# A hybrid decoder layer on one core: seven tiles of x turned in 32-wide blocks on VectorE instead of transposed on TensorE

## What is computed

```python
def in_proj(x, ln_g, w_in):
    u = rmsnorm(x, ln_g) @ w_in                      # 1024 -> 512 + 128 + 128 + 512 + 512
    q, k, v, xl, yg = jnp.split(u, SPLITS, axis=-1)
    ...

q, k, v, xl, yg = in_proj(hp, ln1_g[l], w_in[l])
attn, kw, vw = swa_prompt(rotary(q, pos), rotary(k, pos), v, attn_sinks[l])   # window 128, 8 heads, 2 kv heads
lru_h, cbuf, hT = rglru(xl, conv0, h0, *lru_w)
hp = merge_and_ffn(hp, attn, lru_h, yg, *tail_w)     # output projection, router, 32 experts, top 2
```

## Time and profile before

| | us |
|---|---|
| median of 3 runs | 866.26 |
| the runs | 863.41, 866.26, 869.72 |
| profiled execution, its time | 867.14 |
| profiled execution, its span | 865.4 |
| mean granted clock of TensorE | 0.929 |

### The profile page before, as it was taken

One profiled execution on the slowest core, in us unless ns is written; L12 is line 12 of the kernel. 1 busy time (PEld: TensorE's weight loads), 2 busy tenths in 40 slices (PEclk: granted clock), 3 DMA queues, 4 the chain that ended last, 5 costly groups with the idle time before them and its releaser, 6 DMA issues.

```text
span 865.4 us, 11816 instructions
## 1 busy us (share of the span) xinstructions
PE 752.7 (87%) x4461; PEld 375.7 (43%) x4461; DVE 364.8 (42%) x1023; ACT 239.6 (28%) x556; POOL 140.9 (16%) x193
## 2 busy tenths in 40 slices
PE   6999999599999989899999259999999999999400
PEld 3666665256666645455555223333333333333100
DVE  0556665554458454565565711111111111111087
ACT  2766665400531534111111101111111111111022
POOL 1011001000121121021121221221122211221132
PEclk9999999698999989999999669999999999999855
DMA  9201200210110012611214648999999999992193
GB/s 335 103 25 49 105 7 1 101 53 0 55 37 19 1 48 92 279 73 51 95 50 172 266 115 294 416 395 420 409 404 417 405 420 406 399 376 96 65 388 142
DMA packets 28055, 164.10 MB, mean 190 GB/s; under 512 B 7017, under 2 KB 8193, under 8 KB 17738
## 3 DMA queue, kind: packets, MB, share of 16 engines
q1 hardware_dynamic: 19778, 145.34, 42.4%
q0 software_dynamic: 8080, 17.51, 5.5%
q10 hardware_dynamic: 144, 0.52, 0.2%
HBM read 151.14 MB, written 23.12 MB: 201 GB/s over the span
## 4 chain that ended last, share of the span: by engine, by line
PE 76%; DVE 10%; issue 5%; DMA 4%; ACT 4%; ACTq 0%; POOL 0%; DVEq 0%; SPq 0%; POOLq 0%
PE PS L1772 20%; PE PS L1788 10%; PE PS L1486 7%; PE PS L1623 6%; PE PS L1631 5%; PE PS L1607 4%; PE PS L1598 3%; PE PS L1487 3%; PE PS L1757 3%; PE PS L1515 2%; PE PS L1587 2%; PE PS L1669 2%; PE PS L1471 2%; DMA xin<-in_x 1%; DVE RA L1425 1%
## 5 line engine op out<-in xcount | busy, mean ns | idle before, releaser
L1772 PE MATMUL PS<-BIG,RD 128*32 128x512 f32 x1536 | 171.4, 598 | 0.0
L1772 PEld LDWEIGHTS PS<-BIG,RD 128*32 128x32 f32 x1536 | 47.9, 110 | 105.9 <-issue 105.9
L1788 PE MATMUL PS<-BIG,RD 128*32 128x512 f32 x768 | 87.3, 595 | 0.7 <-ACT RD L915 0.7
L1384 DVE SCALAR_TENSOR_TENSOR RD<-RD,PS 128x256 f32<-128x256 f32 x25 | 10.5, 421 | 177.4 <-ACT RD L898 177.4
L1486 PE MATMUL PS<-BIG,RA 128*128 128x512 f32 x128 | 66.7, 603 | 4.6 <-DMA BIG<-in_wqkv 3.1
L708 POOL DMA_INDIRECT ypair<-RD,pids x25 | 25.3, 1013 | 228.9 <-DVE RD L1400 219.0
L1631 PE MATMUL PS<-BIG 128*128 128x512 f32 x128 | 59.7, 612 | 0.0
L1607 PE MATMUL PS<-RA,BIG 128*128 128x344 f32 x192 | 58.7, 467 | 0.0
L1623 PE MATMUL PS<-BIG 128*128 128x512 f32 x128 | 58.2, 598 | 0.0
L1598 PE MATMUL PS<-RA,BIG 128*128 128x344 f32 x192 | 57.2, 453 | 0.0
L898 ACT ACTIVATE RD<-PS 128x256 f32<-128x256 f32 x25 | 9.6, 385 | 169.0 <-PE PS L1772 161.8
(11 more groups left out here) (265 smaller groups left out, 1024.4 us busy)
## 6 DMA issues: line engine op xcount, KB each, us to landing
BIG<-in_wexp SPq DMA_DIRECT2D x33, 2048.0 KB, 12.7
BIG<-in_wexp SPq DMA_DIRECT2D x33, 1024.0 KB, 13.1
xin<-in_x SPq DMA_DIRECT2D x16, 512.0 KB, 3.4
BIG<-ypair SPq DMA_DIRECT2D x8, 1024.0 KB, 8.6
BIG<-in_wxy SPq DMA_DIRECT2D x4, 1024.0 KB, 4.8
out_y<-RD SPq DMA_DIRECT2D x8, 512.0 KB, 4.2
xtab<-RD SPq DMA_DIRECT2D x7, 512.0 KB, 3.4
BIG<-in_wqkv SPq DMA_DIRECT2D x4, 768.0 KB, 10.1
```

Of the source, the lines that this page charges most:

```text
L1772: o = MM(PS[own, 2 + p2, :], xgT[:, p2, k, own], wgu[expert(n, j) % NG][:, k * 512:(k + 1) * 512], start=(k == 0), stop=(k == KD - 1))
L1788: o = MM(PS[own, 5 + half, :], hT[:, p2, k, own], wdn[expert(n, j) % ND][:, at:at + 512], start=(k == 0), stop=(k == KF - 1))
```

## The change

x of tiles 1 to 7 is loaded twice. The second load (`load_quarters`, four DMAs of 128 KB, runs of 1 KB) puts the quarter q of each token's features on partitions 32q to 32q + 31, four groups of 32 tokens side by side, into a new tile `xp` with two halves. VectorE turns it (`turn`, four instructions of 128x256, f32, each eight 32x32 blocks to a quarter, read with a step of 8 elements) straight into `xT_all`. The features are dealt to partitions in another order for that (partition p has features 8p to 8p + 7), so the rows of `wqkv` and `wxy` and the gain `g1` are laid out on the host in the same order, and the transposes of tiles 0 and 8, which stay on TensorE, read `xin` with a step of 8. ScalarE scales `xT_all` in place for tiles 1 to 7. The quarters of tile 1 are issued ahead of x of tile 1, of the constants and of the sinks; `turn(1)` stands ahead of `variance(0)`, `turn(t + 2)` at the end of pass t. Some semaphores are merged with others.

```diff
@@ sync
+            def load_quarters(t):
+                for q in range(NQ):
+                    src = a["x"][t * P:(t + 1) * P, q * CHUNK_D:(q + 1) * CHUNK_D].rearrange("(j i) e -> i j e", i=STRIP)
+                    dst = xp[STRIP * q:STRIP * q + STRIP, t % 2, :].rearrange("i (j e) -> i j e", e=CHUNK_D)
+                    sp.dma_start(dst, src).then_inc(xp_in[t % 2], 16)
...
+            load_quarters(1)
             load_x(1, 1, P, x_in)
             sp.dma_start(cst[:, K_MASK:], a["cst"][:, K_MASK:]).then_inc(cst_in, 16)
...
             for t in range(2, NT):
-                sp.wait_ge(xT_ps, 2 * t - 2)
+                if t < NPT:
+                    if t >= 3:
+                        sp.wait_ge(xd_ok, t - 2)
+                    load_quarters(t)
+                if t == 2:
+                    sp.wait_ge(xT_ps, 2)
                 sp.wait_ge(x_sq, t - 1)
                 load_x(t, t % 2, P if t < NPT else NDEC, x_in)
@@ scalar
             def evict_x(t, half):
-                act.wait_ge(xT_ps, 2 * t + 1 + half)
+                if by_psum(t):
+                    act.wait_ge(xT_ps, (2 if t else 0) + 1 + half)
+                else:
+                    act.wait_ge(xd_ok, t)
                 for k in range(4 * half, 4 * half + 4):
-                    o = A(xT_all[:, k, t * P:(t + 1) * P], PS[:, 6 if half else 7, (k % 4) * P:(k % 4 + 1) * P], ACT.Copy,
+                    xk = xT_all[:, k, t * P:(t + 1) * P]
+                    o = A(xk, PS[:, 6 if half else 7, (k % 4) * P:(k % 4 + 1) * P] if by_psum(t) else xk, ACT.Copy,
                           scale=g1[:, k:k + 1])
@@ vector
+            def turn(t):
+                dve.wait_ge(xp_in[t % 2], 16 * NQ * ((t + 1) // 2))
+                for j in range(NQ):
+                    at = t * P + j * STRIP
+                    o = V.transpose(xT_all[:, :, at:at + STRIP],
+                                    xp[:, t % 2, j * CHUNK_D:(j + 1) * CHUNK_D].rearrange("p (c k) -> p k c", k=KD))
+                o.then_inc(xd_ok, 1)
+
             for t in range(NT):
                 b = t - 1
                 if b < 0:
+                    turn(1)
                     variance(0)
...
                     V.tensor_tensor(mT_all[:, 0:NFT, b * P:(b + 1) * P], PS[:, 6, :].rearrange("q (a c) -> q a c", a=NFT),
                                     bc(gna[:, :], P), ALU.mult).then_inc(attn_ok, 1)
+                if t + 2 < NPT:
+                    turn(t + 2)
@@ tensor
-                    o = TR(PS[:, 6 if half else 7, (k % 4) * P:(k % 4 + 1) * P], xin[:, t % 2, k * P:(k + 1) * P], ident)
+                    o = TR(PS[:, 6 if half else 7, (k % 4) * P:(k % 4 + 1) * P], xin[:, t % 2, :].rearrange("p (c k) -> p k c", k=KD)[:, k], ident)
...
             qkv(0, range(KD))
-            turn_x(1, 0)
-            turn_x(1, 1)
             qkv(1, range(FIRST))
             turn_qk(0)
             for t in range(1, NT):
                 scores(t - 1)
-                if t + 1 < NT:
-                    turn_x(t + 1, 0)
-                    turn_x(t + 1, 1)
+                if t + 1 == NPT:
+                    turn_x(NPT, 0)
+                    turn_x(NPT, 1)
                 qkv(t, range(FIRST, KD))
```

More of the change, by code:

```diff
@@ L55 @@
 NCOL = NU + NE * MAXC
+NQ = P // STRIP
+CHUNK_D = D_MODEL // NQ
 MAXV = TOPK * TOKENS // (SLOTS + 1) + 1
@@ L206, in build @@
         rinv = RD.cut(N_HEADS)
+        xp = RD.cut(2, D_MODEL)
         RD.phase()
@@ L307, in build @@
         asq_ok = sem("asq_ok")
-        asum_ok = sem("asum_ok")
         drv_ok = sem("drv_ok")
@@ L357, in build @@
         xT2a_ok = sem("xT2a_ok")
-        wr_ok = sem("wr_ok")
         r_ps = sem("r_ps")
@@ L395, in build @@
         g_free = sem("g_free")
-        x3a = sem("x3a")
         gf_in = sem("gf_in")
         x_in = [sem("x_in0"), sem("x_in1")]
+        xp_in = [sem("xp_in0"), sem("xp_in1")]
+        xd_ok = sem("xd_ok")
         x_in2 = [sem("x_in2_0"), sem("x_in2_1")]
@@ L437, in t_bank, with by_psum @@
             return {0: (7, 7), 1: (7, 2)}.get(i, (7, 0))[half]
+        def by_psum(t):
+            return t in (0, NPT)
         def trig(t, at):
@@ L618, in sum_squares @@
                 h = sqa[:, b % 2]
-                nc.gpsimd.tensor_tensor(h[:, 0:2, :], h[:, 0:2, :], h[:, 2:4, :], ALU.add).then_inc(asum_ok, 1)
-                pool.wait_ge(asum_ok, b + 1)
+                nc.gpsimd.tensor_tensor(h[:, 0:2, :], h[:, 0:2, :], h[:, 2:4, :], ALU.add).then_inc(gm0, 1)
+                pool.wait_ge(gm0, b + 2)
                 nc.gpsimd.tensor_tensor(asq[:, b * P:(b + 1) * P], h[:, 0, :], h[:, 1, :], ALU.add).then_inc(asq_ok, 1)
@@ L830, in _ @@
                 o = A(wr[:, k, :], wr[:, k, :], ACT.Copy, scale=g2c[:, k:k + 1])
-            o.then_inc(wr_ok, 1)
+            o.then_inc(drv_ok, 1)
             act.wait_ge(rbc_ok, 1)
@@ L1422, in add_y @@
                 x2 = x2_all[:, t, :]
-                V.scalar_tensor_tensor(x2, yp[:, t % 4, 0:D_MODEL], comb[:, t, 0:1], x2, ALU.mult, ALU.add).then_inc(x3a, 1)
-                dve.wait_ge(x3a, t + 1)
+                V.scalar_tensor_tensor(x2, yp[:, t % 4, 0:D_MODEL], comb[:, t, 0:1], x2, ALU.mult, ALU.add).then_inc(dve_done, dq.up())
+                dve.wait_ge(dve_done, dq.now())
                 V.scalar_tensor_tensor(x2, yp[:, t % 4, D_MODEL:], comb[:, t, 1:2], x2, ALU.mult, ALU.add).then_inc(x3_ok, 1)
@@ L1455, in turn_x @@
                     pe.wait_ge(x_in[t % 2], 16 * (t // 2 + 1))
-                if t == 1:
-                    pe.wait_ge(xs_ok, 2)
-                if t >= 3 and half == 1:
+                if t >= 1 and half == 1:
                     pe.wait_ge(attn_ok, t - 2)
@@ L1507, in values @@
                 pe.wait_ge(ptd_ok, b + 1)
-                pe.wait_ge(xs_ok, 2 * min(b + 2, NT - 1) + 2)
+                if b + 2 >= NPT:
+                    pe.wait_ge(xs_ok, 2 * NPT + 2)
                 if b >= 1:
@@ L1520, in turn_qk @@
                 pe.wait_ge(rot_ok, t + 1)
-                pe.wait_ge(xs_ok, 2 * min(t + 1, NT - 1) + 1)
+                if t + 1 >= NPT:
+                    pe.wait_ge(xs_ok, 2 * NPT + 1)
                 if t >= 1:
@@ L1661, in router @@
                 if i == 0:
-                    pe.wait_ge(wr_ok, 1)
+                    pe.wait_ge(drv_ok, 2)
                     pe.wait_ge(dec_ok, 1)
@@ L1882, in layout, with spread @@
     wqkv = np.concatenate([q, w_in[:, ATTN:QKV]], 1)
+    def spread(m):
+        return m.reshape(P, KD, m.shape[1])
     def tiles(m):
@@ L1887, in layout @@
     xl, yg = w_in[:, QKV:QKV + LRU], w_in[:, QKV + LRU:]
-    wxy = np.stack([tiles(np.concatenate([xl[:, f * P:(f + 1) * P], yg[:, f * P:(f + 1) * P]], 1)) for f in range(NFT)])
+    wxy = np.stack([spread(np.concatenate([xl[:, f * P:(f + 1) * P], yg[:, f * P:(f + 1) * P]], 1)) for f in range(NFT)])
     wg = np.zeros((NFT, P, 2 * P), np.float32)
@@ L1908, in layout @@
         "x": np.concatenate([n["x_prompt"][0], n["x_sample"][:, 0]], 0),
-        "cst": cst, "payload": pay, "g1": n["ln1_g"][0].reshape(KD, P).T, "g2c": n["ln2_g"][0].reshape(KD, P).T, "gna": gna,
+        "cst": cst, "payload": pay, "g1": n["ln1_g"][0].reshape(P, KD), "g2c": n["ln2_g"][0].reshape(KD, P).T, "gna": gna,
         "sinkc": n["attn_sinks"][0][pair][:, None], "sinks": n["attn_sinks"][0], "chp": chp,
@@ L1913, in layout @@
         "b_router": np.concatenate([n["b_router_grp"][0], n["b_router_exp"][0]]),
-        "g2": n["ln2_g"][0], "gf": n["final_g"], "wqkv": tiles(wqkv), "wxy": wxy, "wgate": wg,
+        "g2": n["ln2_g"][0], "gf": n["final_g"], "wqkv": spread(wqkv), "wxy": wxy, "wgate": wg,
         "wout": tiles(np.concatenate([woa, wo[ATTN:]], 0)), "wexp": wexp,
```

## The result

| | before | after |
|---|---|---|
| median, us | 867.74 (4 runs) | 877.26 (4 runs: 871.38, 876.69, 877.82, 880.45) |
| ratio, 95% interval | | 1.0113 (1.0071 to 1.0156) |
| profiled execution, its time | 867.14 | 871.38 |
| profiled execution, its span | 865.4 | 869.6 |
| mean granted clock | 0.929 | 0.936 |

The change makes the kernel slower, by 9.5 us of the medians. I had forecast +3.9 us, 870.2, with a range up to 877.0: the median lies just outside. The profiled execution, with a span of 869.6, looks as if the forecast were right. It is not: that execution is the fastest of the four, and the part of it that the change touches is 9.7 us longer, as the passes show.

What follows compares the result with a forecast made beforehand. The prediction took the chain of VectorE and ScalarE, 16.3 us plus the turn, to bound the passes, near TensorE's 16.5. Start +1.4 and five passes +2.5 made +3.9 on 866.3, so 870.2 us, range 862 to 877.

Steps and rivals of the forecast that it cites:

- the chain: In each tile pass: dependent work of VectorE and ScalarE, 16.3 us without the turn, whose whole time adds to it.
- T: VectorE's time for the four transposes of one tile's turn, taken as 1.6 us.
- rival 1: In the passes: TensorE stays the bound, each of six passes wins up to 0.93 us; 861.7 us; chance 0.12.
- I take half of it, 0.40 us each: In VectorE's turn: the stepped read costs half of 0.1 us, so 0.40 us a transpose and T = 1.6.
- Rival 2: In VectorE's turn: transposes run at half rate, T = 2.5 us; +10.1 in all, 876.4 us; chance 0.14.
- +1.4: At the start: turn(2) waits for its data, so the next scores come at 47.0 instead of 45.59, +1.4 us.
- 28.6 + 1.6, and a little: At the start: the data for turn(2) lands at about 30.5 us, with 0.5 MB more ahead of it.
- the other chain: At the start: late sinks and turn(1) delay the first eviction by 1.8 us, tile 1's projection to 26.0.
- rival 3: In TensorE's gap of 4.2 us in tile 1: the clock falls, +2 us, 872.2 us; chance 0.16.
- signs of being wrong: In the profile after: passes of 16.5, a transpose over 0.5, start moved over 3, or changes after 180 us.

Runs made afterwards that it cites:

- Three kernels with T from 1.3 to 4.2: The changed kernel with transposes read in plain order (T 1.33 us, pass 17.63), unedited (2.12, pass 18.42), and with every transpose done twice (4.22, pass 20.50).
- the early turn: The changed kernel with turn(t + 2) moved ahead of VectorE's wait before the attention output; pass 16.61 us, ratio 0.9993 to the kernel before.
- the second one: The changed kernel run and profiled once more, unedited; ratio 1.0097 to the kernel before, times 874.05 to 877.58 us, profiled span 873.1.

## Why the prediction was wrong

**Right: the chain.** That the turn lies wholly on VectorE's chain, that the chain is 16.3 us and breaks even at 1.1 us of new work, that five passes are hit, pass 1 and pass 7 not. Three kernels with T from 1.3 to 4.2 give 16.3 + T, and the early turn gives the TensorE-bound pass. In the passes rival 1, the gain, failed on the place of the turn alone: with it moved, five passes gave 0.8 each.

**The step that failed in the passes: T, 1.6 against 2.12.** The step of the sum is "I take half of it, 0.40 us each". The operation itself was right at 0.33 to 0.35; the read with step 8 costs 0.20 and not 0.05. The one row I had, L1258, showed 13 ns over 32 elements, 0.4 ns an element; even taken whole it was half of the 0.8 measured over 256. I halved it again, where a long instruction is a better judge than a short one. Five passes then cost 5.0, not 2.5. Rival 2 priced it at 2.5: the truth lay between, and nearer to it.

**The step that failed in the start: +1.4 against +4.6.** The prediction let `scores(1)` hang on `turn(2)`, and `turn(2)` on its data, landed at 30.5; `maxima(0)` came out at 32.1 and `scores(1)` at 47.0, 14.9 later. The last part holds: 50.23 - 35.29 = 14.94. `maxima(0)` was 3.2 late, 0.5 by T and 2.6 by the landing, 33.1. The term that was too small is "28.6 + 1.6, and a little": it priced the quarters at the 400 GB/s of the earlier trace rows, and they moved at 224; and tile 2's own were issued from 20.86 to 22.3, where the load of before went out at 18.39. The Trainium skill's rule of the ports ("SBUF — State Buffer", Door 1: The DMA port swizzle) had given 2.6 us for the quarters of tile 1, and I kept it out of the sum as no row showed it.

The prediction also had a wrong overlap. It let the other chain, over the sinks, the projection of tile 1 and `turn_qk(0)`, be over well before that landing: by its terms the projection of tile 1 starts at 26.0 and `variance(1)` ends at 29.8. It started at 27.69 and ended at 33.17, together with the landing. Of the difference 1.7 is the sinks (2.6 late, not 1.6) and the turn ahead of `variance(0)` (2.1, not 1.6), and 1.7 is rival 3, the clock, after a gap of 5.7 us and not 4.2. I had kept the clock apart as a case of its own with 0.16, but the gap grows with the other two terms. In the profiled execution the two chains tie, so none of these terms alone accounts for the +4.6; in the second one the chain with the clock ended last, by 2.3 us.

**The range.** Its upper end was rival 2 by itself. The median of 877.26 is near rival 2's time, but not by rival 2: T was smaller than its 2.5 and the start was later. Rival 2's own sum has a slip: with T = 2.5 and data at 30.5, `maxima(0)` is at 33.0 and not 33.9, which makes +2.3 for the start and 875.5 in all. Two of the signs of being wrong that I had named came up, a transpose over 0.5 us and a start moved by more than 3.

**Right by chance.** The profiled span, 869.6, within 0.3 of the forecast for a span, is the first stage's +9.7 less the 5.5 by which the rest happened to be shorter in this execution, with a higher clock.

**Covered as said.** The stepped reads of TensorE's own transposes: eight took 1.15 in pass 7 against 1.09. ScalarE's scaling in place: no wait of TensorE for it in the passes. SP's DMAs in the loop: nobody waited after tile 2.

## What to carry to other kernels

Before work moves to an idle engine, find where in its order the idle time is: 2.1 us of turns cost 1.8 a pass behind a wait and nothing ahead of it. Where two bounds lie close (16.3 and 16.5), the room is their distance from the present pass, not the share of time that an engine idles. At the start of a kernel several chains can end together, as the late projection and the late data did here, and then repairing one gives nothing: new loads and new work belong behind what the first results need, and here it was best to leave the first tiles as they were. Before loads are priced at the rate of others, look at how many partitions they go to.

## What the runs showed of the hardware

- A VectorE transpose of 128x256 f32 in 32x32 blocks takes 0.33 to 0.36 us from start to start when its source is contiguous or has a step of 2 elements, and 0.51 to 0.53 with a step of 4 or 8.
- Four loads of 128 KB to 32 partitions each delayed what stood behind them by 2.3 to 5.1 us against the profile of before, the same bytes to 128 partitions by 1.3 (one run). With the DMA engines busy throughout, 224 GB/s were moved from 14 to 18 us in the changed kernel, 399 from 15 to 18 before.
- In the changed kernel the first quarter of tile 3, issued at 24.4, landed 5.8 us later, ahead of the last one of tile 2, which was issued at 22.3 and took 10.8.
- TensorE's granted clock fell to 0.50 (1.2 GHz) after idle stretches of 2.33, 2.40, 3.59 and 5.72 us in three kernels, and stayed at 1.00 (2.4 GHz) after one of 3.70 and three of 2.32. The length of the idle stretch alone does not tell.
- The clock of one stretch of 60 us in a later stage was 0.91 in some executions and up to 1.00 in others, and what lies behind the first stage was some 5 us longer in the former. A single profile's span can be off by more than the change that it is to show; compare the stretch that was changed.
